# Gate logits of two merges computed between attention items and parked in DRAM; the convolution branch moved up beside merge 2

## The chip, the cores and the metric

One core of a Trainium2 chip runs the whole program. The metric is device time in microseconds from start to end of one execution; the lower, the better. Engines: TensorE (PE, its weight loads PEld), VectorE (DVE), ScalarE (ACT), GpSimd (POOL), SyncE (SP), and 16 DMA engines. Each engine runs its own instructions in order and waits on semaphores.

## The reference

Two layers of a hybrid trunk over 512 latent tokens and 256 context tokens, width 1024, in float32. Each layer normalizes its input to `h`, projects it with `w_in`, and feeds three branches of width 512, whose outputs are merged:

```python
def conv_module(val, glu, z, conv_w, conv_b, ln_g, ln_b):
    a = val * jax.nn.sigmoid(glu)
    a = depthwise_conv(a, conv_w) + conv_b
    return jax.nn.silu(layer_norm(a, ln_g, ln_b)) * jax.nn.silu(z)

def merge_branches(ys, gate_logits, w_branch, w_out):
    y = jnp.stack(ys, axis=2)
    proj = jnp.einsum('btnw,nwd->btnd', y, w_branch)
    gates = jax.nn.sigmoid(gate_logits.reshape(gate_logits.shape[0], gate_logits.shape[1], N_BRANCH, D_MODEL))
    return jnp.sum(gates * proj, axis=2) @ w_out

...
    ys = (y_conv, delta_out(o_dn, dz), diff_out(o_da, az))
    x_new = x + gate[:, None] * merge_branches(ys, mgate, w_branch, w_out)
```

Branch 0 is the convolution (31 taps), branch 1 a chunked gated delta rule in both directions, branch 2 differential attention with four heads. The logits `mgate` are columns of `h @ w_in`: they need nothing of the branches. In the last layer only the latent tokens go on, so most products there have 512 columns and not 768.

## The kernel before

**Items and units.** `schedule()` writes out one list of items, and every engine's program walks this list in order. `units_of(item)` gives the weight units of an item: blocks of 128 x 1024 weights, streamed from DRAM in the order of the list. A dense product is made of three float32r products (high x high, high x low, low x high), so each unit is loaded by SP into `raw`, rounded to `wH` by ScalarE (L754), and its rest `wL` formed by GpSimd (L1684), both in a function `ahead`, which runs up to three units before the unit in use; the ring has four slots, and a slot is reloaded when TensorE is done with the unit before. The products are made in `dense` (L419): a unit has 24 stationary blocks, against 768 columns (two matmuls each) in layer 0 and 512 in most of layer 1.

**Merges.** `merge_steps(l, n)` is four times: gate unit, gate unit, branch unit. A gate's logits stay in a PSUM bank until ScalarE writes their sigmoid to `sg` (L1042). The branch unit gives two products, which VectorE multiplies by `sg` (L1570); for n = 1 into `mT`, otherwise into the single buffer `gm`, which GpSimd adds to `mT` (L1785). The operands of a branch product are `yH` and `yL`, one pair of buffers for all three branches.

**Attention.** The items of head h are `att_steps`: "sc" (scores of a query tile, L466, VectorE's maxima, ScalarE's exponentials L777) and "pv" (transposition L443 of the mixed softmax `Pa`, then the values' product L479 of the tile before). VectorE mixes the softmax of tile i (L1253, L1256) in the "sc" item of tile i+1, the last one in the last "pv". Six query tiles in layer 0, four in layer 1. Between them, `weave` puts a list `side[h]`: the projections of the next head (three units and five short items) and pieces of the merges. Each head ends with "aout": unit az, a sum over the head (L435), ScalarE's reciprocal root and Silu into `vr` (L1157), VectorE's product, `yH` (L1159) and `yL` (L1690).

```python
side = [weave(heads[1], fill[6:]), heads[2], heads[3], merge_steps(l, 2)[:2]]
```

**Tail.** Behind attention stand, one after another: the rest of merge 2 (six gates, four branches) with the layer norm's sum and variance ("lnsum", "lnvar") among it, four z units of the convolution branch, merge 0 (eight gates, four branches), then the output units. In "z" GpSimd scales `acc` by `rsc` (L1794), ScalarE applies Silu (L1068), VectorE multiplies (L1607), ScalarE writes `yH` (L1073), GpSimd `yL` (L1690). VectorE makes the convolution (L1279) in small steps, one at each of many items. Twenty modulation units ("ada", L510) are woven over the whole list in layer 0.

## Time and profile before

| | |
|---|---|
| three runs | 2342.32, 2342.53 and 2440.72 us; median 2342.53 |
| profiled execution | 2335.97 us, span of its instructions 2334.2 us, mean granted clock 0.891 |
| PE busy | 1940.2 us (83%) |
| DVE, ACT, POOL busy | 1077.4 (46%), 986.2 (42%), 778.2 (33%) us |
| DMA | 157.95 MB, mean 68 GB/s |
| weight units | 226, 512 KB each |

The stretches of the table of busy time below are cut where TensorE has finished the sum of an "aout" item. In layer 0 head 0 of attention begins at 635.8 us, head 1 at 760.5, head 2 at 854.5, head 3 at 955.3, and attention's last sum ends at 1033.8; in layer 1 these are 1833.0, 1922.5, 1990.0, 2057.7 and 2111.6. The tail of layer 0 ends at 1285.5 and that of layer 1 at 2273.4. In a row of the timeline stand start, duration, engine, line and operation, and in brackets the engine's idle time before it with what ended it.

### The profile page before, as it was taken

The page shows a single profiled execution, that of the slowest core. Times are in us where ns is not written, and L with a number is a line of the kernel's source. Part 1 is how long each engine was busy: PE and PEld are TensorE (multiplying, and loading weights), DVE is VectorE, ACT ScalarE, POOL GpSimd, SP SyncE. Part 2 cuts the span into 40 slices and gives each one's busy share as a digit, 9 for nine tenths or more (in the row PEclk, how much of TensorE's full clock was granted, in tenths as well). Part 3 has the DMA queues.
Part 4 walks back from the last instruction along what each step waited for, and adds up shares of the span by engine and source line. Part 5 has one row for each costly group of instructions (what it writes and reads, how often), then busy time and mean ns, then how long its engine had stood idle before and what let it go on. Part 6 is the DMA issues. An engine that isn't in the chain of part 4 may idle for free. (4 is left out here: it accounts for less than half of the span.)

```text
span 2334.2 us, 28547 instructions
## 1 busy us (share of the span) xinstructions
PE 1940.2 (83%) x11444; PEld 1623.3 (70%) x11444; DVE 1077.4 (46%) x1592; ACT 986.2 (42%) x1320; POOL 778.2 (33%) x428
## 2 busy tenths in 40 slices
PE   7677896999999877769999767778498997768997
PEld 6665785887887656558888646657487775656876
DVE  3444557358666656421100233547758665541002
ACT  4345652335353544433232234565235545544331
POOL 0122233444434222223554311315145431213562
PEclk8588996799999978779999887989699998889998
DMA  4222222321211101011221312212121210101223
GB/s 176 76 70 64 63 82 73 120 71 46 73 64 55 55 28 46 28 37 54 73 71 65 135 64 64 68 59 91 38 64 56 80 55 28 37 19 58 96 97 111
DMA packets 66194, 157.95 MB, mean 68 GB/s; under 512 B 5328, under 2 KB 28176, under 8 KB 65808
## 3 DMA queue, kind: packets, MB, share of 16 engines
q1 hardware_dynamic: 33264, 122.46, 15.8%
q10 hardware_dynamic: 32800, 33.66, 4.4%
q8 instruction: 93, 1.52, 0.3%
q14 instruction: 37, 0.30, 0.0%
HBM read 145.52 MB, written 10.58 MB: 67 GB/s over the span
## 5 line engine op out<-in xcount | busy, mean ns | idle before, releaser
L1684 POOL TENSOR_TENSOR wL<-raw,wH 128x1024 fp32r<-128x1024 f32 x210 | 523.5, 2496 | 1059.7 <-ACT wH L754 1059.5
L419 PE MATMUL banks<-hH,wH 128*128 128x512 f32 x1984 | 598.6, 363 | 70.4 <-issue 32.9
L419 PE MATMUL banks<-hL,wH 128*128 128x512 f32 x1984 | 581.0, 354 | 0.0
L419 PE MATMUL banks<-hH,wL 128*128 128x512 f32 x1984 | 580.0, 354 | 0.0
L419 PEld LDWEIGHTS banks<-hH,wH 128*128 128x128 f32 x1984 | 327.6, 192 | 135.6 <-issue 74.0
L754 ACT ACTIVATE wH<-raw 128x1024 fp32r<-128x1024 f32 x226 | 237.8, 1054 | 399.3 <-DMA raw<-wstream 399.0
L419 PEld LDWEIGHTS banks<-hL,wH 128*128 128x128 f32 x1984 | 326.2, 192 | 57.2 <-issue 3.9
L419 PEld LDWEIGHTS banks<-hH,wL 128*128 128x128 f32 x1984 | 324.4, 191 | 54.6
L1279 DVE SCALAR_TENSOR_TENSOR acc<-padc,vecs,acc 128x783 f32<-128x783 f32 (+1 forms) x240 | 292.6, 1274 | 0.0
L1570 DVE TENSOR_TENSOR gm<-banks,sg 128x768 f32<-128x768 f32 (+1 forms) x32 | 26.4, 824 | 279.3 <-PE banks L419 218.6
L510 PE MATMUL banks<-wH,csx 128*128 128x128 f32 x384 | 125.7, 350 | 17.4 <-DVE wL L1214 12.1
L777 ACT ACTIVATE Pa<-banks,stat 128x768 f32<-128x768 f32 (+1 forms) x80 | 64.5, 812 | 155.7 <-DVE stat L1240 155.4
L510 PE MATMUL banks<-wL,csx 128*128 128x128 f32 x384 | 123.1, 344 | 0.0
L510 PEld LDWEIGHTS banks<-wH,csx 128*128 128x128 f32 x384 | 99.4, 259 | 20.3 <-issue 13.5
L419 PE MATMUL banks<-yH,wH 128*128 128x512 f32 (+1 forms) x288 | 90.3, 368 | 21.0 <-issue 21.0
L510 PEld LDWEIGHTS banks<-wL,csx 128*128 128x128 f32 x384 | 100.3, 261 | 0.8 <-issue 0.8
L443 PE MATMUL banks<-cons,Pa 128*128 128x128 f32 x208 | 37.5, 323 | 71.5 <-DVE Pa L1256 71.5
L760 ACT ACT_TABLE_LOAD x52 | 66.7, 1283 | 58.3 <-PE banks L435 57.3
L419 PE MATMUL banks<-yL,wH 128*128 128x512 f32 (+1 forms) x288 | 88.5, 362 | 0.0
L419 PE MATMUL banks<-yH,wL 128*128 128x512 f32 (+1 forms) x288 | 88.4, 361 | 0.0
L466 PE MATMUL banks<-kh,qh 64*128 64x256 f32 (+1 forms) x288 | 64.5, 566 | 26.6 <-ACT vr L1157 14.8
L443 PEld LDWEIGHTS banks<-cons,Pa 128*128 128x128 f32 x208 | 28.0, 164 | 82.1 <-issue 81.0
(249 smaller groups left out, 2621.8 us busy)
## 6 DMA issues: line engine op xcount, KB each, us to landing
raw<-wstream SPq DMA_DIRECT2D x226, 512.0 KB, 3.4
E<-g_rows ACTq DMA_DIRECT2D x16, 384.0 KB, 6.9
egb<-eg_rows ACTq DMA_DIRECT2D x20, 256.0 KB, 4.0
inb<-intra_rows ACTq DMA_DIRECT2D x20, 256.0 KB, 4.6
xs<-xT SPq DMA_DIRECT2D x1, 3072.0 KB, 15.4
intra_rows<-E ACTq DMA_DIRECT2D x8, 384.0 KB, 3.3
xs<-xT ACTq DMA_DIRECT2D x1, 3072.0 KB, 13.4
x_between<-xs ACTq DMA_DIRECT2D x8, 384.0 KB, 3.3
```

Source lines behind the costliest of these rows:

```text
L419: last = pe.matmul(out[:, a:b], w, m[:, kt, a:b], start=(kt == 0 and j == 0), stop=(kt == kts - 1 and j == 2))
L443: last = pe.transpose(out[:, c * P:(c + 1) * P], src[:, c * P:(c + 1) * P], ident)
L466: last = pe.matmul(outs[m][:, o:o + b - a], q_[r, qt * P:(qt + 1) * P], k_[r, a:b], start=True, stop=True)
L510: last = pe.matmul(out[:, 0:P], csx[:, 4 * kt:4 * kt + P], w[i][:, kt * P:(kt + 1) * P], start=(kt == 0 and j == 0), stop=(kt == KT - 1 an ...
L754: act.activation(wH[w % RING][:, :], raw[w % RING][:, :], ACT.Copy).then_inc(*tick("act", "hi", v))
L760: ins = act.activation(dst[:, 0:n], place[readkey][:, 0:n], ACT.Ln, bias=e, scale=scale)
L777: act.activation(Pa[i][m][:, 0:w], place[key][:, 0:w], ACT.Exp, bias=stat[:, i, 2 + m:3 + m], accum_out=stat[:, i, 4 + m:5 + m]).then_inc( ...
L1279: ins = dve.scalar_tensor_tensor(acc[:, t, 0:W], padc[:, t, k:k + W], w, acc[:, t, 0:W], ALU.mult, ALU.add)
L1570: dve.tensor_tensor(dst, place[(u, j)][:, 0:n], sg[j][:, 0:n], ALU.mult).then_inc(*tick_read("dve", (u, j)))
L1684: pool.tensor_tensor(wL[w % RING][:, :], raw[w % RING][:, :], wH[w % RING][:, :].bitcast(F32), ALU.subtract).then_inc(*tick("pool", "lo", v))
```

## The change

The sixteen gate units of merges 2 and 0 become items "park", and are woven into heads 1, 2 and 3: four, five and seven. ScalarE copies the logits to `sg` and sends them to DRAM; two parks share the two buffers. Behind attention `park_in` brings two tiles of logits back at a time into four buffers `sgin`, and `sigmoids` is applied in place. The order behind attention is now: "lnsum", z unit 0, "lnvar", z unit 1, the first "ynorm" (the second half of what was "z"), then four branches of merge 2 with the other z units and "ynorm" items between them, then four branches of merge 0. The convolution branch has operand buffers of its own, `yH0` and `yL0`, and merges 2 and 0 have two product buffers `gms`. VectorE makes a convolution step at every gate or park item.

```diff
@@ -118,13 +118,15 @@
                  for h in range(NT)]
         att = [att_steps(l, h) for h in range(NT)]
         fill = merge_steps(l, 1)
-        side = [weave(heads[1], fill[6:]), heads[2], heads[3], merge_steps(l, 2)[:2]]
+        park = [("park", l, n, d) for n in (2, 0) for d in range(KT)]
+        side = [weave(heads[1], fill[6:]), weave(heads[2], park[:4]), weave(heads[3], park[4:9]), park[9:]]
         mid = weave(heads[0], fill[:6])
         for h in range(NT):
             mid += weave(att[h], side[h]) + [("aout", l, h)]
-        rest = merge_steps(l, 2)[2:]
-        mid += rest[:1] + [("lnsum", l)] + rest[1:4] + [("lnvar", l)] + rest[4:]
-        mid += [("z", l, t) for t in range(NT)] + merge_steps(l, 0)
+        mid += [("lnsum", l), ("z", l, 0), ("lnvar", l), ("z", l, 1), ("ynorm", l, 0)]
+        for p in range(4):
+            mid += [("branch", l, 2, p)] + [("z", l, p + 2)] * (p < 2) + [("ynorm", l, p + 1)] * (p < 3)
+        mid += [("branch", l, 0, p) for p in range(4)]
         out += weave(mid, late)
         out += [("out", l)]
     return out
...
...
@@ -320,8 +325,12 @@
 
         padc = arena("padc", [P, NT, PADW], PADC)
         acc = arena("acc", [P, NT, ACCW], ACC0)
-        sqc = [arena("sqc_%d" % i, [P, ACCW], 16 * T3 + i * 3264) for i in range(2)]
+        sqc = [arena("sqc_%d" % i, [P, ACCW], 26 * T3 + i * 3264) for i in range(2)]
         rsc = arena("rsc", [P, TOK], 20 * T3)
+        yH0 = arena("yH0", [P, NT, TOK], 22 * T3, F32R)
+        yL0 = arena("yL0", [P, NT, TOK], 26 * T3, F32R)
+        sgin = [sg[0], sg[1]] + [arena("sgin%d" % i, [P, TOK], (30 + i) * T3) for i in range(2)]
+        gms = [gm, arena("gm1", [P, TOK], 21 * T3)]
         zt = [arena("zt_%d" % i, [P, TOK], 16 * T3 + i * T3) for i in range(4)]
 
         qh = [arena("qh_%d" % i, [P, TOK], (16 + i) * T3) for i in range(2)]
@@ -337,6 +346,7 @@
         csb = arena("csb", [P, KT, 2], 31 * T3 + 1024)
         cs32 = arena("cs32", [P, KT, 2], 31 * T3 + 1088)
 
+        pscr = nc.dram_tensor("parked_logits", (DEPTH, 2, KT, P, TOK), F32, kind="Internal").ap()
         xscr = nc.dram_tensor("x_between", (P, KT, TOK), F32, kind="Internal").ap()
         gscr = nc.dram_tensor("g_rows", (2, NC, NT, P), F32, kind="Internal").ap()
         egscr = nc.dram_tensor("eg_rows", (2, NC, NT, P), F32, kind="Internal").ap()
@@ -655,7 +665,7 @@
                 elif k == "glu":
                     unit(("val", l, it[2]), "val")
                     unit(("glu", l, it[2]), "glu")
-                elif k == "gate":
+                elif k in ("gate", "park"):
                     unit(units_of(it)[0], "gate")
                 elif k == "branch":
                     n, p = it[2], it[3]
@@ -664,7 +674,7 @@
                     for j in range(2):
                         out = product(pe, (u, j), w)
                         pe.wait_ge(*done("y", n, l, NT - 1))
-                        last = dense(u, out, yH, yL, segs(w), NT, j * P, 2 * P)
+                        last = dense(u, out, yH if n else yH0, yL if n else yL0, segs(w), NT, j * P, 2 * P)
                         last.then_inc(*tick("pe", "pe", (u, j)))
                     got[("pe", u)] = got[("pe", (u, 1))]
                 elif k == "lnsum":
@@ -782,6 +792,22 @@
                 for d in range(2):
                     act.dma_start(E[h % 2][:, d, :, :], gscr[d, :, h, :].unsqueeze(0).to_broadcast([P, NC, P])).then_inc(
                         *tick("e_in%d" % (h % 2), "Ein", l, h, d, by=16))
+
+            def park_in(l, n_, p):
+
+                n = ntok(l, "gate")
+                for d in (2 * p, 2 * p + 1):
+                    act.wait_ge(*done("park", l, n_, d))
+                    act.wait_ge(*done("park", l, 0, KT - 2 + d % 2))
+                    act.dma_start(sgin[d % 4][:, 0:n], pscr[l, n_ // 2, d, :, 0:n]).then_inc(
+                        *tick("park_in%d" % (d % 4), "gin", l, n_, d, by=16))
+
+            def sigmoids(l, n_, p):
+
+                n = ntok(l, "gate")
+                for d in (2 * p, 2 * p + 1):
+                    act.wait_ge(*done("gin", l, n_, d))
+                    act.activation(sgin[d % 4][:, 0:n], sgin[d % 4][:, 0:n], ACT.Sigmoid).then_inc(*tick("act", "gsig", l, n_, d))
 
             def scan_in(l, s):
 
@@ -1040,11 +1066,36 @@
                         act.wait_ge(*done(*last_sg[d % 2]))
                     last_sg[d % 2] = ("gm", l, n_, d)
                     act.activation(sg[d % 2][:, 0:n], place[u][:, 0:n], ACT.Sigmoid).then_inc(*tick_read("act", u))
+                elif k == "park":
+                    n_, d = it[2], it[3]
+                    n = ntok(l, "gate")
+                    u = units_of(it)[0]
+                    ahead(u)
+                    act.wait_ge(*done("pe", u))
+                    act.wait_ge(*done(*last_sg[d % 2]))
+                    last_sg[d % 2] = ("park", l, n_, d)
+                    act.activation(sg[d % 2][:, 0:n], place[u][:, 0:n], ACT.Copy).then_inc(*tick_read("act", u))
+                    act.wait_ge(*done("read", u, 0))
+                    act.dma_start(pscr[l, n_ // 2, d, :, 0:n], sg[d % 2][:, 0:n]).then_inc(
+                        *tick("park_out%d" % (d % 2), "park", l, n_, d, by=16))
                 elif k == "branch":
+                    n_, p = it[2], it[3]
                     ahead(units_of(it)[0])
+                    if n_ == 2 and p == 0:
+                        sigmoids(l, 2, 0)
+                    if n_ == 2 or n_ == 0 and p < 3:
+                        sigmoids(l, n_ if p < 3 else 0, (p + 1) % 4)
+                    if n_ == 2 or n_ == 0 and p < 2:
+                        for d in (2 * p, 2 * p + 1):
+                            act.wait_ge(*done("gm", l, n_, d))
+                        park_in(l, n_ if n_ == 2 and p < 2 else 0, (p + 2) % 4)
                 elif k in ("lnsum", "lnvar"):
                     n = ntok(l, "cz")
                     W = ACCW if n == TOK else SEQ
+                    if k == "lnsum":
+                        act.wait_ge(*done("pe", ("o", l, 3, ntok(l, "aq") // P - 1)))
+                        park_in(l, 2, 0)
+                        park_in(l, 2, 1)
                     for t in ((0, 1) if k == "lnsum" else (2, 3)):
                         act.wait_ge(*done("xc", l, t))
                         if t >= 2:
@@ -1058,10 +1109,12 @@
                     u = ("cz", l, t)
                     ahead(u)
                     act.wait_ge(*done("pe", u))
-                    act.wait_ge(*done("rsc", l))
                     if t >= 2:
                         act.wait_ge(*done("y32", 0, l, t - 2))
                     act.activation(zt[t % 2][:, 0:n], place[u][:, 0:n], ACT.Silu).then_inc(*tick_read("act", u))
+                elif k == "ynorm":
+                    t = it[2]
+                    n = ntok(l, "cz")
                     act.wait_ge(*done("xn", l, t))
                     for a, b in segs(n):
                         o = HALO if a else 0
@@ -1069,8 +1122,8 @@
                                          scale=vecs[:, l, V_LG + t:V_LG + t + 1],
                                          bias=vecs[:, l, V_LB + t:V_LB + t + 1]).then_inc(*tick("act", "lns", l, t, a))
                     act.wait_ge(*done("y32", 0, l, t))
-                    act.wait_ge(*done("pe", ("branch2", l, 3)))
-                    act.activation(yH[:, t, 0:n], zt[2 + t % 2][:, 0:n], ACT.Copy).then_inc(*tick("act", "yh", 0, l, t))
+                    act.wait_ge(*done("yl", 2, l, NT - 1))
+                    act.activation(yH0[:, t, 0:n], zt[2 + t % 2][:, 0:n], ACT.Copy).then_inc(*tick("act", "yh", 0, l, t))
                 elif k == "qunit":
                     h, kind = it[2], it[3]
                     u = (kind, l, h)
@@ -1257,7 +1310,7 @@
                                          ALU.mult, ALU.add).then_inc(*tick("dve", "mixp", l, h, qt))
 
             added = set()
-            last_gm = [None]
+            last_gm = [None, None]
             conv_done = [0]
 
             def conv(l, n):
@@ -1559,22 +1612,21 @@
                         u = ("branch%d" % n_, l, p)
                         gu = ("gate%d" % n_, l, d)
                         dve.wait_ge(*done("pe", (u, j)))
-                        dve.wait_ge(*done("read", gu, 0))
+                        dve.wait_ge(*(done("read", gu, 0) if n_ == 1 else done("gsig", l, n_, d)))
                         if n_ == 1:
                             dst = mT[:, d, 0:n]
                         else:
-                            dst = gm[:, 0:n]
-                            if last_gm[0]:
-                                dve.wait_ge(*done(*last_gm[0]))
-                            last_gm[0] = ("gadd", l, n_, d)
-                        dve.tensor_tensor(dst, place[(u, j)][:, 0:n], sg[j][:, 0:n],
+                            dst = gms[j][:, 0:n]
+                            if last_gm[j]:
+                                dve.wait_ge(*done(*last_gm[j]))
+                            last_gm[j] = ("gadd", l, n_, d)
+                        dve.tensor_tensor(dst, place[(u, j)][:, 0:n], (sg[j] if n_ == 1 else sgin[d % 4])[:, 0:n],
                                           ALU.mult).then_inc(*tick_read("dve", (u, j)))
                         got[("gm", l, n_, d)] = got[("read", (u, j), 0)]
                         if n_ == 1:
                             got[("gadd", l, 1, d)] = got[("gm", l, n_, d)]
                 elif k in ("gate", "qunit", "vunit"):
-                    if k != "gate" or it[2] == 1:
-                        conv(l, 1)
+                    conv(l, 1)
                 elif k == "lnsum":
                     conv(l, 2 * CK)
                     n = ntok(l, "cz")
@@ -1592,7 +1644,7 @@
                             got[("xc", l, t)] = got[("read", key, 0)]
                         else:
                             ins.then_inc(*tick("dve", "xc", l, t))
-                elif k == "z":
+                elif k == "ynorm":
                     t = it[2]
                     n = ntok(l, "cz")
                     dve.wait_ge(*done("read", ("cz", l, t), 0))
@@ -1687,7 +1739,8 @@
             def lowy(n_, l, h, n, y32):
 
                 pool.wait_ge(*done("yh", n_, l, h))
-                pool.tensor_tensor(yL[:, h, 0:n], y32[:, 0:n], yH[:, h, 0:n].bitcast(F32), ALU.subtract).then_inc(*tick("pool", "yl", n_, l, h))
+                hi, lo = (yH, yL) if n_ else (yH0, yL0)
+                pool.tensor_tensor(lo[:, h, 0:n], y32[:, 0:n], hi[:, h, 0:n].bitcast(F32), ALU.subtract).then_inc(*tick("pool", "yl", n_, l, h))
                 got[("y", n_, l, h)] = got[("yl", n_, l, h)]
 
             pool.memset(csx[:, KT * 4:].bitcast(F32), 0.0).then_inc(*tick("pool", "csx0"))
@@ -1773,7 +1826,7 @@
                         pool.memset(padc[:, :, :], 0.0).then_inc(*tick("pool", "padz", l))
                     for u in units_of(it):
                         ahead(u)
-                elif k == "gate":
+                elif k in ("gate", "park", "z"):
                     ahead(units_of(it)[0])
                 elif k == "branch":
                     n_, p = it[2], it[3]
@@ -1782,12 +1835,11 @@
                     if n_ != 1:
                         for d in (2 * p, 2 * p + 1):
                             pool.wait_ge(*done("gm", l, n_, d))
-                            pool.tensor_tensor(mT[:, d, 0:n], mT[:, d, 0:n], gm[:, 0:n],
+                            pool.tensor_tensor(mT[:, d, 0:n], mT[:, d, 0:n], gms[d % 2][:, 0:n],
                                                ALU.add).then_inc(*tick("pool", "gadd", l, n_, d))
-                elif k == "z":
+                elif k == "ynorm":
                     t = it[2]
                     n = ntok(l, "cz")
-                    ahead(units_of(it)[0])
                     pool.wait_ge(*done("rsc", l))
                     for a, b in segs(n)[::-1]:
                         o = HALO if a else 0
```

## Rows read from the trace of the kernel before

**Rows 1.** Busy time by stretch, layer 0: length, busy and count, clock, DMA share

```profile
635.80:760.50 124.70, 118.72 (x695) 98.79 (x694) 83.00 (x100) 54.08 (x74) 43.78 (x18) 0.99 0.19 60
760.50:854.50 94.00, 72.51 (x391) 57.17 (x390) 52.61 (x78) 43.09 (x63) 25.26 (x12) 0.89 0.13 40
854.50:955.30 100.80, 80.47 (x409) 64.15 (x408) 55.72 (x80) 44.22 (x65) 26.77 (x13) 0.80 0.13 42
955.30:1033.80 78.50, 57.83 (x307) 46.76 (x306) 32.26 (x62) 33.09 (x51) 13.69 (x6) 0.83 0.10 34
1033.80:1055.50 21.70, 11.12 (x48) 9.59 (x49) 2.93 (x3) 8.19 (x8) 5.97 (x3) 0.69 0.06 22
1055.50:1285.50 230.00, 230.00 (x1319) 198.63 (x1317) 23.68 (x39) 66.60 (x75) 109.52 (x56) 1.00 0.21 68
```

**Rows 2.** Busy time by stretch, layer 1, the same columns

```profile
1833.00:1922.50 89.50, 84.44 (x413) 65.93 (x412) 59.70 (x72) 40.86 (x53) 32.29 (x15) 0.96 0.18 59
1922.50:1990.00 67.50, 53.20 (x269) 41.29 (x268) 35.44 (x52) 34.76 (x47) 16.51 (x10) 0.90 0.10 32
1990.00:2057.70 67.70, 53.91 (x267) 42.02 (x266) 35.57 (x52) 34.77 (x47) 15.84 (x10) 0.85 0.10 31
2057.70:2111.60 53.90, 37.78 (x179) 28.14 (x178) 21.01 (x38) 26.70 (x37) 7.96 (x5) 0.87 0.09 30
2111.60:2128.40 16.80, 7.99 (x25) 6.43 (x26) 2.13 (x3) 7.34 (x8) 5.52 (x4) 0.70 0.10 32
2128.40:2273.40 145.00, 143.40 (x617) 115.07 (x615) 14.93 (x22) 53.24 (x63) 83.98 (x46) 1.00 0.28 91
```

**Rows 3.** Waits of PE, layer 0, 760.5 to 1033.8 (total us, times, longest)

```profile
PE banks L443 <- DVE Pa L1256: 38.0, 11, 5.7
PE banks L466 <- ACT vr L1157: 10.3, 2, 5.1
PE banks L510 <- ACT vr L1157: 5.1, 1, 5.1
```

**Rows 4.** Waits of PE, layer 1, 1922.5 to 2111.6

```profile
PE banks L443 <- DVE Pa L1256: 29.2, 7, 5.7
PE banks L466 <- issue: 5.7, 2, 2.8
PE banks L466 <- ACT vr L1157: 4.5, 1, 4.5
```

**Rows 5.** Busy time by stretch: one gate unit of layer 0, two of layer 1

```profile
983.41:991.84 8.43, 8.43 (x49) 7.44 (x49) 2.34 (x6) 5.20 (x8) 3.40 (x2) 1.00 0.19 62
2224.29:2235.17 10.88, 10.88 (x50) 9.01 (x48) 0.69 (x1) 2.72 (x3) 7.12 (x5) 1.00 0.31 96
```

**Rows 6.** Timeline of PE, layer 0: the first matmul of merge 2's first branch

```profile
1044.38 0.77 PE L419 MATMUL banks<-yH,wH 128*128 128x512 f32 x1 [10.60 <-issue]
```

**Rows 7.** Timeline of PE: the layer norm's sum, layer 0 and layer 1

```profile
1055.51 5.12 PE L435 MATMUL banks<-acc,ones 128*128 128x512 f32 x15
...
2128.26 3.59 PE L435 MATMUL banks<-acc,ones 128*128 128x512 f32 x8
```

**Rows 8.** Timeline of ACT, layer 1: the convolution branch's last heads, then a gate

```profile
2209.41 0.63 ACT L1073 ACTIVATE yH<-zt 128x512 fp32r<-128x512 f32 x1 [0.81 <-DVE zt L1607]
2209.94 1.04 ACT L754 ACTIVATE wH<-raw 128x1024 fp32r<-128x1024 f32 x1
...
2216.67 0.63 ACT L1073 ACTIVATE yH<-zt 128x512 fp32r<-128x512 f32 x1 [0.81 <-DVE zt L1607]
...
2218.27 1.28 ACT L1042 ACT_TABLE_LOAD   x1
2219.56 0.60 ACT L1042 ACTIVATE sg<-banks 128x512 f32<-128x512 f32 x1
```

**Rows 9.** Timeline of ACT, layer 0: one issue of a DMA

```profile
1309.82 0.33 ACTq L1172 DMA_DIRECT2D x_between<-xs  x1
```

**Rows 10.** DMA issues: KB each, median us to landing

```profile
intra_rows<-E ACTq DMA_DIRECT2D x8, 384.0 KB, 3.3
```

3 lines of the change are left out of this document (added).

## Prediction

> **What bounds the kernel now.** I read the table of busy time by stretch first, cut at the output item of each attention head [rows 1, 2]. It shows where TensorE isn't full. Layer 0's tail, from "lnsum" to the end of merge 0, has 230.0 us with PE busy for 230.0, clock 1.00. Layer 1's tail lacks 1.6 us in 145.0. Head 0 of attention, with ten weight units among its items, is nearly full as well: 6.0 us idle in 124.7. Heads 1, 2 and 3 have four, four and three units, and leave 21.5, 20.3 and 20.7 us idle, at clocks of 0.89, 0.80 and 0.83; the 21.7 us between attention and the tail leave 10.6. Layer 1 looks the same: 14.3, 13.8, 16.1 and 8.8 us. So the kernel is bound by TensorE, except where the softmax chain runs with too little beside it.
>
> What a stretch loses I call its excess: length less PE busy, plus busy time by (1 - granted clock), an estimate of what the lower of the two levels (1.2 for 2.4 GHz) costs. Layer 0: heads 21.5+8.0, 20.3+16.1, 20.7+9.8, together 96.4 us, and 10.6+3.4 = 14.0 after them. Layer 1: 14.3+5.3, 13.8+8.1, 16.1+4.9, together 62.5, and 8.8+2.4 = 11.2 [rows 1, 2]. The table of waits says what ends the idle time [rows 3, 4]: the transposition in a "pv" item waits for VectorE's mixed softmax (38.0 us in 11 waits, 3.5 each; layer 1 29.2 in 7, 4.2 each), and the second product behind an "aout" item waits until ScalarE has read that item's banks (15.4 us in three; layer 1 10.2 in three, with those put down to issue).
>
> **The change part by part.** TensorE's work stays the same: every unit, product and column. The sum is made of idle time and clock.
>
> (1) *Gates moved.* Sixteen gate units a layer lie between attention items, where two did; 14 leave a tail that was full, at 8.43 us each in layer 0 and 10.88/2 = 5.44 in layer 1 [rows 5]. Heads 1, 2 and 3 get 4, 5 and 7 of them, in place of 0, 0 and 2. Written out item by item, a "pv" waits only if no unit stands between it and the "sc" item in which VectorE mixes its softmax, or if VectorE has a head sum's result to wait for first. In layer 0 those are three in head 1 (the fourth to sixth query tile), one in head 2 (the fifth), none in head 3; in layer 1 one, one and none. At today's means [rows 3, 4] that is 4 x 3.5 = 13.8 us and 2 x 4.2 = 8.3. The bank wait stays whole (15.4 and 10.2), since the same products stand behind "aout". Of the other small waits (62.5-38.0-15.4 = 9.1 us; layer 1 4.8) I keep 3 and 2, head 0's level. Idle after: 32.2 and 20.5. The clock falls behind idle time: today 33.9 us of clock loss on 62.5 idle (0.54), in layer 1 18.3 on 44.2 (0.41) [rows 1, 2]; by the same ratios 17.4 and 8.4. Excess after: 49.6 and 28.9. **Gain 46.8 + 33.6 = 80.4 us.** A second way, from head 0: three heads like it (7.2 us of excess each, 8.5 in layer 1) and the bank waits with their clock share (23.7, 14.4) give 45.3 and 39.9, a gain of 74.
>
> (2) *What a park adds.* On ScalarE a Copy in place of a Sigmoid of the same size and a DMA issue of 0.33 us [rows 9]. The wait for that write's landing stands two parks later, at least two units (16.9 or 10.9 us) away, against 3.3 us for 384 KB to DRAM on this queue [rows 10]. Behind ScalarE's wait for the unit stand only exponentials that TensorE hasn't prepared either. Cost 0; with the cover gone, 3.3 us a time. On VectorE convolution steps move up with the parks and end in head 2, so head 3's softmax meets none. On GpSimd and SP the weights pass in the new order; ScalarE and GpSimd are at most 46% and 27% busy in these heads [rows 1]. The reads are issued from "lnsum" on, about two branches ahead of use.
>
> (3) *Handover.* The first branch of merge 2 waits 10.6 us for its operand [rows 6]. After the change "lnsum" (5.1 us; 3.6 in layer 1 [rows 7]) and z unit 0 stand before it, and z unit 1 too: this stall and its 3.4 us of clock go. Next late is the variance sum, which waits for squares: in layer 0 it starts 13.5 us behind attention's last sum, and has them; in layer 1 after 9.0 us, where I count 2.3 us of wait (bounds 0 and today's 8.8 [rows 2]).
>
> (4) *The shorter tail.* Merge 0 needs the convolution branch, whose heads go one by one through ScalarE, GpSimd and VectorE. Today this cycle is 7.26 us in layer 1 (2209.41 to 2216.67 [rows 8]). Woven between the branches of merge 2 it takes on two table loads (2 x 1.28), another wH (1.04), two sigmoids (1.2) and two DMA issues (0.7): 12.7 us, while TensorE's work per cycle, a branch and a z unit, is 10.9. TensorE has done "lnsum", two z units and "lnvar" 20 us behind attention's end; the first y comes some 6 us later (end of wH 2210.98 to end of yH 2217.30 [rows 8]), the last one three cycles on, at 64. TensorE has six more units (32.6 us) and asks for it at 53. The last cycle has no z unit in it, so I take 10 us of wait and not 11. With the 2.3 and 0.3 of clock loss per us of idle, as at the handover today (2.4 on 8.8): 16.0 us of excess, against 11.2+1.6 today. In layer 0 the steps that grow with the columns (12.7 less loads, wH, its wL and the issues: at most 6 us, by at most 768/512) add under 3 us: 15.7, under TensorE's 16.9. Only the last y is late there, about 2.7 us, with the clock 4.0. What the second product buffer of merges 2 and 0 gives before the output units I take at 0. **Layer 0: 14.0 - 4.0 = 10; layer 1: 12.8 - 16.0 = -3.**
>
> In this chain the change adds switches of ScalarE's table. The rows show a load of 1.28 us whose sigmoid starts 0.01 us behind it: a switch costs 1.28 here [rows 8].
> The Trainium skill (ScalarE: Activation LUTs, "What ACT_TABLE_LOAD costs") puts a drain of about 1.38 us on each switch; by that rule the cycle of layer 1 would be 15.5 us and that of layer 0 18.5, and the sum some 13 us worse. The trace doesn't agree.
>
> **Sum.** 80.4 + 10 - 3 = 87 us. The profiled execution took 2335.97 us (span 2334.2), which gives 2249; the runs' median is 2342.53, 6.6 more, so I forecast 2255, 3.7% down.
>
> **The rivals.**
> *Full cover* (0.10): no "pv" waits, and layer 1's chain keeps up. That is 22 us of waits, 11 of clock and 16 of the tail more: 2206. For it: head 0's clock of 0.99. Against: head 0 still idles 6 us, with ten units.
> *Only head 3 gains* (0.15): in heads 1 and 2 the head sums and rotations keep the waits where they are. Layer 0 gains 30.5-9.4 = 21, layer 1 21.0-7.3 = 14, the rest 7: 42 us, 2300. Against it: head 0, with the same small items.
> *Costly switches* (0.05): each table load drains ScalarE before the next step. At one more load's length per switch (1.28 [rows 8]), eight in layer 1's chain and the last cycle of layer 0: 13 us, 2268.
> *Slower: the trip to DRAM* (0.04): ScalarE, in order, stands in a DMA wait with the softmax behind it. All 64 transfers at 3.3 us would be 211 us: 2466. It decides from 1.4 us per transfer on the path (87/64). That needs landings several times longer than today's [rows 10], as two units lie between a write and the wait for it.
> *No effect* (0.02): the stretches keep their idle time although units lie in them: 2342.
> The forecast keeps 0.64.
>
> **Range and chances.** The forecast's own spread is the number of "pv" waits (2 to 8 a layer, 5 us each with clock) and layer 1's tail (0 to 20 us): 2225 to 2285. The range 2222 to 2300 takes in costly switches and nearly all of "only head 3"; full cover's end and the slower case stay out. 2% (47 us) is about what a measurement of this kernel can tell from no change; that line is at 2296. Faster 0.80 (forecast, full cover, switches, a little of the third), within 0.16, slower 0.04.
>
> **What would show it.** Heads 1 to 3 longer by their gates, with PE idle 10 to 14, 8 to 11 and 5 to 7 us and a clock of 0.92 or more; the bank wait unchanged in each; no wait behind the last head's sum; one wait of some 10 us at the first branch of merge 0 in layer 1, ended by GpSimd's yL, and 3 us in layer 0. I am wrong if merge 2's branches wait for sigmoids, if weights come late behind the new traffic, or if heads 1 and 2 still idle 20 us.

## The result, and the profile after

The changed kernel takes **2265.92 us** (median of four runs, 2263.15 to 2271.35) beside 2343.4 for the kernel before on the same chip: ratio 0.9681, 95% interval 0.9658 to 0.9704. The ratio is of runs in the fast state alone; one of the four of the kernel before (2440.72 us) was slower and isn't in it. The forecast was 2255, in a range of 2222 to 2300. The two profiled executions have spans of 2269.6 and 2334.2 us, 64.6 apart; the account below is made on them. The medians lie about 77 us apart, since the profiled execution of the kernel before was 7 us faster than its median and that of the changed kernel 5 us slower; the gains by spans below come out smaller by that much.

Busy time by stretch of the changed kernel, layer 0: head 0, heads 1 to 3, the tail from "lnsum" to the end of merge 0, and the time up to the output units. Columns as in [rows 1].

```profile
635.56:765.09 129.53, 120.86 (x695) 100.28 (x694) 82.96 (x101) 54.21 (x74) 42.94 (x18) 0.97 0.19 58
765.09:890.66 125.57, 109.53 (x600) 90.16 (x599) 56.97 (x80) 51.34 (x73) 37.52 (x17) 0.90 0.20 64
890.66:1019.66 129.00, 114.90 (x647) 95.50 (x646) 58.01 (x80) 53.20 (x75) 40.22 (x18) 0.93 0.21 69
1019.66:1123.30 103.64, 94.22 (x565) 78.89 (x565) 43.35 (x64) 39.91 (x60) 28.35 (x12) 0.98 0.25 83
1123.30:1246.50 123.20, 119.01 (x660) 101.57 (x658) 25.52 (x38) 63.67 (x71) 77.63 (x43) 0.97 0.34 112
1246.50:1260.85 14.35, 0.35 (x3) 0.24 (x3) 11.32 (x13) 8.03 (x11) 6.28 (x3) 0.55 0.75 282
```

Layer 1: heads 1 to 3 and the tail. Compare [rows 2].

```profile
1886.54:1972.47 85.93, 73.98 (x363) 57.34 (x363) 35.98 (x52) 41.38 (x55) 25.56 (x14) 0.92 0.20 62
1972.47:2060.99 88.52, 80.68 (x387) 62.67 (x386) 35.76 (x52) 43.05 (x57) 28.63 (x15) 0.94 0.22 69
2060.99:2127.75 66.76, 61.05 (x299) 47.51 (x299) 23.11 (x38) 31.04 (x44) 20.52 (x10) 0.97 0.30 91
2127.75:2210.30 82.55, 74.64 (x305) 57.76 (x303) 16.43 (x25) 51.98 (x63) 56.16 (x36) 0.96 0.39 127
```

Length less the first busy column is the idle time: 16.0, 14.1 and 9.4 us in the heads of layer 0 (before 21.5, 20.3 and 20.7), 12.0, 7.8 and 5.7 in layer 1 (14.3, 13.8 and 16.1). The units are where they should be: PE's matmuls in the three heads of layer 0 went from 391, 409 and 307 to 600, 647 and 565. The excess, worked out as in the prediction (in the column "after", idle time and clock loss):

| stretch | before | predicted | after | gain predicted | gain measured |
|---|---|---|---|---|---|
| heads 1 to 3, layer 0 | 96.4 | 49.6 | 39.5 + 20.9 = 60.4 | 46.8 | 36.0 |
| heads 1 to 3, layer 1 | 62.5 | 28.9 | 25.5 + 12.6 = 38.1 | 33.6 | 24.4 |
| handover and tail, layer 0 | 14.0 | 4.0 | 4.2 + 3.6 = 7.8 | 10 | 6.2 |
| handover and tail, layer 1 | 12.8 | 16.0 | 7.9 + 3.0 = 10.9 | -3 | 1.9 |
| head 0, layer 0 | 7.2 | 7.2 | 8.7 + 3.6 = 12.3 | 0 | -5.1 |
| before the output units, layer 0 | 11.9 | 11.9 | 14.0 | 0 | -2.1 |

Together 61 of the 64.6 us; the stretches outside the table give 1 us, and the rest is within the rounding of the clock column. What PE waited for in heads 1 to 3, layer 0:

```profile
PE banks L429 <- ACT vr L1210: 10.3, 2, 5.1
PE banks L453 <- DVE Pa L1309: 7.9, 2, 4.2
PE banks L476 <- ACT vr L1210: 5.1, 1, 5.1
PE banks L453 <- ACT Pa L787: 4.7, 1, 4.7
PE banks L489 <- ACT Pa L787: 3.4, 2, 2.4
PE banks L453 <- ACT adar L844: 2.4, 2, 2.0
```

and in layer 1:

```profile
PE banks L453 <- DVE Pa L1309: 10.8, 2, 8.0
PE banks L476 <- issue: 5.9, 2, 3.1
PE banks L476 <- ACT vr L1210: 4.6, 1, 4.6
```

The first line of the first list says: products of L429 (a weight unit) waited twice for banks that ScalarE's `vr` step of L1210 had to read, 10.3 us in all, 5.1 at most. The wait for VectorE's softmax fell from 38.0 us in 11 to 7.9 in 2 [rows 3], and in layer 1 from 29.2 in 7 to 10.8 in 2 [rows 4]. The wait for az's banks (ACT vr) stands as it was, 5.1 us each time in layer 0. The wait of 10.6 us at merge 2 [rows 6] is gone. New in the list is a wait for "adar", ScalarE's copy of an ada unit's result.

### The profile page after: what moved, and what is told of

The parts are those of the page before. It is cut to its first block and busy times, and to the rows that moved or that the text cites. A ratio compares the mean times of both kernels' runs of the same rounds, so it can differ in the third digit from the quotient of the medians.

```text
span 2269.6 us, 28683 instructions
## 1 busy us (share of the span) xinstructions
PE 1919.4 (85%) x11444; PEld 1605.1 (71%) x11444; DVE 1103.4 (49%) x1592; ACT 1009.9 (44%) x1354; POOL 778.2 (34%) x428
## 5 line engine op out<-in xcount | busy, mean ns | idle before, releaser
L429 PE MATMUL banks<-hH,wH 128*128 128x512 f32 x1984 | 604.2, 366 | 83.5 <-issue 31.8
L429 PE MATMUL banks<-hL,wH 128*128 128x512 f32 x1984 | 584.6, 356 | 0.0
L429 PE MATMUL banks<-hH,wL 128*128 128x512 f32 x1984 | 584.1, 356 | 0.0
L429 PEld LDWEIGHTS banks<-hH,wH 128*128 128x128 f32 x1984 | 331.1, 194 | 151.6 <-issue 75.5
L429 PEld LDWEIGHTS banks<-hL,wH 128*128 128x128 f32 x1984 | 329.2, 193 | 57.5 <-issue 4.1
L429 PEld LDWEIGHTS banks<-hH,wL 128*128 128x128 f32 x1984 | 327.3, 192 | 54.7
L1332 DVE SCALAR_TENSOR_TENSOR acc<-padc,vecs,acc 128x783 f32<-128x783 f32 (+1 forms) x240 | 304.3, 1325 | 0.0
L520 PE MATMUL banks<-wH,csx 128*128 128x128 f32 x384 | 118.7, 336 | 11.1 <-DVE wL L1267 11.0
L520 PE MATMUL banks<-wL,csx 128*128 128x128 f32 x384 | 117.4, 333 | 0.0
L520 PEld LDWEIGHTS banks<-wH,csx 128*128 128x128 f32 x384 | 94.8, 247 | 14.0 <-issue 12.5
L429 PE MATMUL banks<-yH,wH 128*128 128x512 f32 (+1 forms) x288 | 89.8, 366 | 11.0 <-issue 11.0
L429 PE MATMUL banks<-yL,wH 128*128 128x512 f32 (+1 forms) x288 | 87.7, 358 | 0.0
L429 PE MATMUL banks<-yH,wL 128*128 128x512 f32 (+1 forms) x288 | 87.6, 358 | 0.0
L453 PE MATMUL banks<-cons,vb 128*128 128x128 f32 x48 | 12.1, 425 | 81.7 <-ACT vb L926 81.7
L770 ACT ACT_TABLE_LOAD x52 | 66.7, 1283 | 32.2 <-PE banks L445 31.5
L1409 DVE TENSOR_SCALAR c<-pad,vecs 128x769 f32<-128x769 f32 (+1 forms) x24 | 46.1, 1922 | 65.3 <-ACT pad L913 65.3
L1290 DVE TENSOR_REDUCE stat<-banks 128x1 f32<-128x768 f32 (+1 forms) x80 | 64.1, 842 | 26.2 <-PE banks L476 26.2
```

The lines of the kernel that those rows point to most:

```text
L429: last = pe.matmul(out[:, a:b], w, m[:, kt, a:b], start=(kt == 0 and j == 0), stop=(kt == kts - 1 and j == 2))
L453: last = pe.transpose(out[:, c * P:(c + 1) * P], src[:, c * P:(c + 1) * P], ident)
L520: last = pe.matmul(out[:, 0:P], csx[:, 4 * kt:4 * kt + P], w[i][:, kt * P:(kt + 1) * P], start=(kt == 0 and j == 0), stop=(kt == KT - 1 an ...
L770: ins = act.activation(dst[:, 0:n], place[readkey][:, 0:n], ACT.Ln, bias=e, scale=scale)
L1290: dve.tensor_reduce(stat[:, i, m:m + 1], place[key][:, 0:w], AX_X, ALU.max).then_inc(*tick("dve", "mx", l, h, qt, m))
L1332: ins = dve.scalar_tensor_tensor(acc[:, t, 0:W], padc[:, t, k:k + W], w, acc[:, t, 0:W], ALU.mult, ALU.add)
```

## The experiments

Twelve kernels ran, each in three rounds beside the kernel before, in groups of four that shared a chip (its median 2338.5, 2338.99 and 2338.71 us there). Ratios are to the kernel before; the changed kernel has 0.9681 (0.9658 to 0.9704). Lines of code are cut where "..." stands.

### Gates and tail, each alone

First the tail in its new order with the gates still in it:

```diff
-        side = [weave(heads[1], fill[6:]), weave(heads[2], park[:4]), weave(heads[3], park[4:9]), park[9:]]
+        side = [weave(heads[1], fill[6:]), heads[2], heads[3], merge_steps(l, 2)[:2]]
...
+            mid += g2[2 * p:2 * p + 2] * (p > 0) + [("branch", l, 2, p)]
```

> The new tail alone: the convolution branch has its own operand buffers and its items stand beside merge 2, but no gate is parked; the gate units stay before their branches as in the kernel before. My theory (most of the gain is made by units that fill idle time between attention items, the rest at the handover): the heads stay as they were, the wait of 10.6 us behind the last head's sum and its clock loss go in layer 0, most of 11 us in layer 1, and the convolution chain is hidden by the gates beside it: about 2318 us, 25 less than before. Rival: the gain came from the tail's order and buffers, the parked gates only moved work from one full place to another: 2266 to 2285. Second rival: the tail gives nothing alone: 2343.

Measured: 2307.79 us, 0.9871 (0.9853 to 0.9888), 10 us under the expectation. The heads didn't stay as they were, though no gate moved: in layer 0 heads 0 and 1 are 4.2 and 3.1 us longer than before, head 2 is 8.7 shorter (92.1 for 100.8) and head 3 3.7. The ada units had moved here too, see below, and one of them (some 2 us) out of head 2; that this is the cause was not run by itself. Its tail in layer 0 has no idle time:

```profile
1029.00:1260.00 231.00, 231.00 (x1325) 200.19 (x1324) 25.81 (x43) 74.03 (x84) 113.95 (x58) 1.00 0.21 67
```

Then the gates parked, with the tail in its old order:

```diff
...
+        mid += [("lnsum", l), ("branch", l, 2, 0), ("branch", l, 2, 1), ("lnvar", l), ("branch", l, 2, 2), ("branch", l, 2, 3)]
+        for t in range(NT):
+            mid += [("z", l, t), ("ynorm", l, t)]
...
```

> The parked gates with the tail in the old order: sum, two branches, variance, two branches, then the four heads of the convolution branch in a row, then merge 0. My theory: PE idle in the heads as in the changed kernel; behind attention a wait of 5 us comes back (the sum covers half of 10.6), and in layer 1 the four z units (5.4 us each) are shorter than the chain's cycle (7.3 us), so merge 0 waits some 8 to 10 us instead of 6.8; in layer 0 hardly anything else: 2275 to 2285 us. Rival (the order of the tail carries the gain): above 2310. Rival (the order is worth nothing): 2266.

Measured: 2297.97 us, 0.9818 (0.9799 to 0.9836), 13 us above the expectation's upper end. Its heads are those of the changed kernel; its tails, layer 0 and 1:

```profile
1120.90:1254.80 133.90, 118.89 (x645) 100.11 (x644) 24.83 (x37) 58.76 (x67) 76.26 (x42) 0.95 0.31 102
2140.90:2236.30 95.40, 77.68 (x305) 59.95 (x303) 16.98 (x25) 47.03 (x59) 55.89 (x36) 0.89 0.33 110
```

15.0 and 17.7 us idle, where the changed kernel has 4.2 and 7.9. The wait of some 5 us for merge 2's operand came back, as expected (5.5 and 5.4); what was missed is the wait at merge 0, 9.2 us in layer 0, where next to none was expected, and 11.6 in layer 1. The two parts add up: 1.29% and 1.82% make 3.11, beside 3.19 for both. A tail without its gates no longer covers the convolution branch's chain, so the new order is worth some 30 us there.

### Which pv items wait

Units put directly before the pv items of heads 1 and 2 (the same units in all):

```diff
...
+            gap = {6: [[q], [k, qs], [v], [qr, units[0]], [ks, units[1]], [vt, units[2]]],
+                   4: [[q, k], [qs, v], [qr, ks, units[0]], [vt, units[1]]]}[n]
+            for qt in range(n):
+                out += [("sc", l, h, qt + 1)] * (qt + 1 < n) + gap[qt] + [("pv", l, h, qt)]
...
```

> The changed kernel with the side items of heads 1 and 2 placed by hand, in both layers: the same items, but a weight unit stands directly before each pv item where the order allows it, the small items (head sums, rotations, turn) ahead of it. My theory (what is left idle in these heads is pv items without a unit before them): the 7.9 us of layer 0 and the 10.8 us of layer 1 that TensorE waits for the mixed softmax go, with their clock loss: 25 to 30 us less than the changed kernel, about 2240. Rival (the rest is due to banks not yet read by ScalarE, whose place in the order I don't change): 2266 within 5 us.

Measured: 2260.67 us, 0.9668 (0.9645 to 0.969), not to be told from the changed kernel, and near the rival's value, not my 2240. Waits of PE in its heads 1 to 3, layer 0:

```profile
PE banks L489 <- ACT vr L1223: 15.4, 3, 5.1
PE banks L442 <- ACT Pa L800: 7.8, 4, 2.0
```

Head 1 has 10.6 us idle for 16.0, head 2 13.9 for 14.1. No pv waits for VectorE any more, as expected, but now the units (L442) wait for banks that ScalarE hasn't read. Here the place of the units decided which item waits, and most of the idle time stayed.

### Where the ada units stand

The late ada units of layer 0 are woven over a list that the four new "ynorm" items make longer (130 places for 126), so that they stand up to one item later than before in head 0, one or two in head 1 and two or three in heads 2 and 3. Spread as in the kernel before:

```diff
-        out += weave(mid, late)
+        groups = []
+        for it in mid:
+            if it[0] == "ynorm":
+                groups[-1].append(it)
+            else:
+                groups.append([it])
+        out += [it for g in weave(groups, [[it] for it in late]) for it in g]
```

> The changed kernel, with its late ada units spread as in the kernel before: the four new ynorm items don't count as places in the list over which they are woven. My theory of head 0 in layer 0, which got 4.8 us longer (129.5 for 124.7): the new items shift the ada units among the attention items, and two of them now stand before pv items of head 0. Then head 0 takes 125 us again, the wait for ScalarE's adar (1.4 us) goes, and the time is some 5 us down, 2261. Rival: the parked traffic or the Copy instead of Sigmoid disturbs head 0 (it can't from a later place in ScalarE's order, but weights come earlier), then it stays at 129.5.

Measured: **2251.96 us**, 0.9616 (0.9592 to 0.964), better than the changed kernel beyond both intervals, and 14 us where 5 were expected. Heads 0 to 3 of layer 0:

```profile
635.80:760.50 124.70, 119.48 (x695) 99.61 (x694) 85.37 (x101) 54.08 (x74) 42.54 (x18) 0.97 0.19 60
760.50:877.20 116.70, 104.22 (x601) 86.86 (x600) 60.70 (x80) 51.48 (x73) 38.23 (x17) 0.96 0.21 68
877.20:1002.60 125.40, 112.37 (x649) 93.58 (x648) 58.38 (x80) 53.46 (x75) 40.55 (x18) 0.96 0.21 71
1002.60:1108.60 106.00, 96.78 (x565) 80.95 (x565) 42.98 (x64) 39.82 (x60) 28.23 (x12) 0.94 0.24 81
```

Head 0 takes 124.7 us again. That isn't chance: in seven other kernels here with the changed kernel's spacing it takes 128.0 to 130.4 us, and in the two at the end that have the old one 124.6 and 124.9 (in the kernel before with Silu first, old spacing too, 127.3 with no more idle time, at a clock of 0.96 for 0.99). The excess of heads 1 to 3 is 16.6 + 17.5 + 15.0 = 49.2 us, where the changed kernel has 60.4: 34.7 us idle for 39.5, and 14.5 of clock loss for 20.9. The other way round, with these units taken out of heads 1 to 3 and put behind "lnsum" (one is left, at the start of head 1):

```diff
...
+            out += weave(mid[:cut], late[:6]) + mid[cut:end] + weave(mid[end:], late[6:])
...
```

> The changed kernel, with the ada units that lay in heads 1 to 3 of layer 0 moved behind lnsum, into the tail. My theory: where ada units stand decides how much idle time the heads have; the earlier spacing gained 14 us, as its units stood before pv items. With none of them in heads 1 to 3 the pv waits that they covered come back, some 2 us of unit and its switch each, 11 units: heads 1 to 3 shorter by the units' own 24 us but with 10 or more us more idle time and clock loss, the tail 24 us longer with no wait at merge 0; 2270 to 2285 in all. Rival: ada units among attention items cost more than they cover (each makes a head's items wait for ScalarE's adar); then the heads' idle time stays or falls and the time is under 2262.

Measured: 2257.28 us, 0.9646 (0.9612 to 0.9679): what the rival expected, and not the 2270 of my theory. Heads 1 to 3 of layer 0:

```profile
759.20:874.50 115.30, 100.78 (x551) 82.14 (x549) 57.99 (x74) 47.88 (x67) 30.07 (x14) 0.91 0.18 56
874.50:991.30 116.80, 104.12 (x579) 85.71 (x578) 53.99 (x72) 48.76 (x67) 30.45 (x14) 0.96 0.18 58
991.30:1089.20 97.90, 89.70 (x513) 74.53 (x513) 37.89 (x58) 36.43 (x54) 20.99 (x9) 0.95 0.22 72
```

The heads' excess is 23.6 + 16.8 + 12.7 = 53.1: less than the changed kernel's 60.4, more than the 49.2 with the units in the old places. The idle time alone is 35.4 us here, 39.5 in the changed kernel and 34.7 in the old places: ada units in the old places covered next to nothing, and in the new places they cost some 4 us. I had held that any ada unit covers some idle time; that fell. That a unit at the wrong item delays it by its own work and its copy on ScalarE is my reading of the waits for "adar" (2.4 us), not shown by a run.

### The wait for az's banks

Silu of az ahead of the reciprocal root in "aout", in the changed kernel and in the one before:

```diff
-                    rsqrt(None, at1[1], 1.0 / P, eps, ("aors", l, h), ("oss", l, h), n)
                     act.wait_ge(*done("pe", u))
                     act.activation(vr[:, 0:n], place[u][:, 0:n], ACT.Silu).then_inc(*tick_read("act", u))
+                    rsqrt(None, at1[1], 1.0 / P, eps, ("aors", l, h), ("oss", l, h), n)
```

> The changed kernel, with the Silu of az moved ahead of the reciprocal root in each aout item, so that the product behind it gets its banks earlier. My theory: the wait for ScalarE's reading of these banks (5.1 us three times in layer 0, some 3.4 three times in layer 1) is a loss of its own, beside the pv waits, and carries its share of the clock: idle time of heads 1 to 3 falls by 15 and 10 us, excess by some 23 and 14, and the time from 2266 to about 2232. Rival: ScalarE is the chain behind aout anyway, and the time reappears as a wait of the next pv for VectorE's softmax or ScalarE's exponentials; then less than 12 us are gained and the pv waits grow by what the bank wait loses.

Measured: 2260.2 us, 0.9645 (0.9624 to 0.9665), 6 us less than the changed kernel by the medians, the intervals just touching; the rival expected that, and my theory 34 us.

> The kernel before, with the same edit (Silu of az ahead of the reciprocal root in aout). If the bank wait is independent of how many gate units lie in the heads, as the prediction had it, this gains the same 25 us of idle time and a share of the clock, some 35 us: 2305 beside 2338. If the chain of the softmax takes it up, which is more likely here as nothing else stands behind aout, under 15 us: above 2324.

Measured: 2339.81 us, 0.9993 (0.9974 to 1.0013): no change. PE behind the "aout" of head 2 in layer 0, first in the kernel before, then with the edit:

```profile
961.96 2.93 PE L466 MATMUL banks<-kh,qh 64*128 64x512 f32 x8 [5.14 <-ACT vr L1157]
969.96 1.30 PE L443 MATMUL banks<-cons,Pa 128*128 128x128 f32 x5 [5.07 <-DVE Pa L1256]
```

```profile
959.17 1.56 PE L466 MATMUL banks<-kh,qh 64*128 64x512 f32 x8 [1.74 <-ACT at L760]
970.26 1.09 PE L443 MATMUL banks<-cons,Pa 128*128 128x128 f32 x4 [9.52 <-DVE Pa L1256]
```

The bank wait falls by 3.4 us and the next pv's grows by 4.5: the transposition starts at the same time (14.6 and 14.3 us behind the head's sum). It was slack in front of the softmax. With units between, a part of it is real: heads 1 and 2 of layer 0 became 6.6 and 6.8 us shorter in the changed kernel, while a unit's wait of 6.4 us for ScalarE's exponentials took the place of one of the three.

### What sets the tail's chain

First the table switches: Sigmoid in place of both Silu of the z and ynorm steps, so that ScalarE switches no table between them and the gates' sigmoids (the convolution branch's activation is then another).

```diff
-                    act.activation(zt[t % 2][:, 0:n], place[u][:, 0:n], ACT.Silu)...
+                    act.activation(zt[t % 2][:, 0:n], place[u][:, 0:n], ACT.Sigmoid)...
...
```

> The changed kernel with Sigmoid in place of both Silu functions of the convolution branch, so that ScalarE needs no table switch between its steps and the gates' sigmoids in the tail (this changes what is computed, and nothing else of the order). My theory (the last cycles of the convolution chain are what merge 0 waits for, with two loads of 1.28 us in each): layer 1's cycle falls from 12 to about 9.5 us, under TensorE's 10.9, and the wait of 6.8 us at merge 0 goes to 2 or less, layer 0's 4.2 to 3: 8 to 10 us less than the changed kernel. If a switch cost a drain too, twice that. Rival (the wait is GpSimd's, its wL and sums in order): no change within 3 us.

Measured: 2270.19 us, 0.9705 (0.969 to 0.9721): nothing gained. ScalarE's loads between these steps are gone, and `yH` still comes every 11.9 us (2147.63, 2159.58 and 2171.51 us). The wait at merge 0, layer 1, in the changed kernel and in this one:

```profile
2186.77 0.77 PE L429 MATMUL banks<-yH,wH 128*128 128x512 f32 x1 [6.77 <-issue]
```

```profile
2183.30 0.77 PE L429 MATMUL banks<-yH,wH 128*128 128x512 f32 x1 [6.58 <-issue]
```

GpSimd in the changed kernel, one cycle of the chain:

```profile
2165.04 2.40 POOL L1736 TENSOR_TENSOR wL<-raw,wH 128x1024 fp32r<-128x1024 f32 x1
2167.39 2.55 POOL L1838 TENSOR_TENSOR mT<-mT,gm 128x512 f32<-128x512 f32 x2
2169.90 2.39 POOL L1736 TENSOR_TENSOR wL<-raw,wH 128x1024 fp32r<-128x1024 f32 x1
2172.24 1.09 POOL L1846 TENSOR_TENSOR acc<-acc,rsc 128x512 f32<-128x512 f32 x1
2175.71 1.30 POOL L1743 TENSOR_TENSOR yL<-zt,yH 128x512 fp32r<-128x512 f32 x1 [2.38 <-ACT yH L1126]
```

It is busy for 9.7 us and waits 2.4 for one round through ScalarE and VectorE: 11.9 us from one yL (2163.79) to the next, with small overlaps. So I took the two additions (L1838) from it and gave them to VectorE:

```diff
...
-                            pool.tensor_tensor(mT[:, d, 0:n], mT[:, d, 0:n], gms[d % 2][:, 0:n], ...
+                            dve.tensor_tensor(mT[:, d, 0:n], mT[:, d, 0:n], gms[d % 2][:, 0:n], ...
```

> The changed kernel, with the additions of merges 2 and 0 to mT on VectorE in place of GpSimd. My theory now: in layer 1's tail GpSimd's order of work (a wL of 2.4, two additions of 1.27, a wL of 2.4, xn 1.1, yL 1.3) sets the cycle of the convolution branch, not ScalarE. Without the additions it falls by some 2.5 us per head: the wait of 6.8 us at merge 0 in layer 1 shrinks to under 1.5, layer 0's 4.2 to about 3 (it is put down to adar), and the time falls by some 7 to 10 us, 2257. Rival: ScalarE's order (sigmoids, wH, norm steps, yH) sets it, and the wait stays within 1.5 us of 6.8.

Measured: 2264.69 us, 0.9669 (0.9639 to 0.9698), not to be told from the changed kernel by its time. In the trace the wait is nearly halved, the cycles are 12.2, 10.4 and 8.2 us, and the tail of layer 1 is 3.5 us shorter:

```profile
2179.48 0.76 PE L429 MATMUL banks<-yH,wH 128*128 128x512 f32 x1 [3.69 <-issue]
```

GpSimd's order does bind, but the wait was expected under 1.5 us and is 3.7: both engines' operations got longer where they met. Two such additions took VectorE 2.06 us at 2203.49, and 4.13 us here:

```profile
2160.84 2.87 POOL L1741 TENSOR_TENSOR wL<-raw,wH 128x1024 fp32r<-128x1024 f32 x1
```

```profile
2160.12 4.13 DVE L1631 TENSOR_TENSOR mT<-mT,gm 128x512 f32<-128x512 f32 x2
```

The same trace has a second gain that I hadn't expected: PE's wait before the output units fell from 11.1 to 9.0 us in layer 0 and from 10.7 to 7.6 in layer 1. With 3.1 us at merge 0 that is 8 of the 9 us by which the profiled span is shorter; the medians, 1 us apart with intervals of some 14 us, can't confirm it.

### The trip to DRAM

Each parked gate written twice, both writes awaited:

```diff
...
+                    act.dma_start(pscr2[l, n_ // 2, d, :, 0:n], sg[d % 2][:, 0:n]).then_inc(
+                        *tick("park_twice%d" % (d % 2), "park2", l, n_, d, by=16))
...
```

> The changed kernel, with every parked gate written to DRAM a second time (to another tensor, on the same queue); the buffer is reused, and the reads begin, only when both writes have landed. The output is the same. The prediction had the price of a park at 0, since two units lie between a write and the wait for it: then the time stays within 4 us of 2266, as 32 more DMA issues on ScalarE and 11 MB are beside TensorE's work. Rival, the trip to DRAM: the landings take up what is gained; 32 more transfers at 3 to 4 us would add tens of us, 2290 or more, and weights would come late.

Measured: 2274.17 us, 0.9716 (0.9684 to 0.9748), 8 us more than the changed kernel by the medians, where at most 4 were expected, with overlapping intervals, and a profiled span of 2270.3 beside 2269.6. By the medians that is a quarter of a microsecond for each of 32 writes; no stretch of the trace shows it, so whether it is there stays open. The second writes of layer 0 (384 KB each) land 4.8 us behind their issue in the median.

### Together

The ada units' old spacing, Silu first and the additions on VectorE, with the units before the pv items too, and without them:

> What gained by itself, together: ada units spread as before, units placed directly before the pv items of heads 1 and 2, Silu of az ahead of the reciprocal root, additions of merges 2 and 0 on VectorE. If the gains add up (14 + 5 + 6 + 6 us by their medians) it gives 2266 - 31 = 2235. If they are the same idle time counted twice (a wait removed by one returns as the next one in the chain of the softmax), about the best of them, 2250.

Measured: 2244.39 us, 0.9591 (0.9556 to 0.9625), between the 2235 of a plain sum and the 2250 of the best edit alone.

> As the run before, without the placing of units before the pv items. 2266 - 26 = 2240 if the gains add up; beside the run before it shows what the placing is worth once no product behind aout waits for az's banks: 5 us, or less if the ada units have already given head 1 its cover.

Measured: **2232.93 us**, 0.9534 (0.9498 to 0.9569), the fastest, 7 us under the plain sum's 2240, 33 us below the changed kernel and 106 below the one before. The three edits together give more than what they gave alone by their medians (14 + 6 + 1), which with intervals of some 10 us each is no contradiction to a plain sum. The placing of units, 5 us by itself and inside the intervals, costs 11 on top of them (the intervals of the two ratios overlap by a hair, but the slowest of the four runs without it, 2234.44, lies below the fastest with it, 2239.82). Heads 1 and 2, layer 0, of the fastest:

```profile
761.40:873.20 111.80, 103.33 (x599) 86.50 (x598) 60.93 (x80) 50.23 (x73) 38.12 (x17) 0.95 0.22 71
873.20:992.70 119.50, 110.46 (x647) 92.26 (x646) 60.46 (x80) 52.07 (x75) 39.52 (x18) 0.97 0.23 74
```

8.5 and 9.0 us idle in heads 1 and 2. With the units placed they are 13.1 each, and what PE waits for there is a unit's banks behind ScalarE's exponentials, 20.7 us in five waits over heads 1 to 3:

```profile
PE banks L448 <- ACT Pa L806: 20.7, 5, 6.4
```

## Why the prediction was right, and where it was off

The forecast's case held, and its time lies 11 us above. By the spans the sum of 87 us became 64.6, by the medians about 77.

(1) *Gates moved.* Right in kind: heads 1, 2 and 3 gain, most where most gates went. The idle time was mis-sized, 39.5 us for 32.2 in layer 0 and 25.5 for 20.5 in layer 1, and the signs that the prediction named for it were missed in layer 0: 16.0, 14.1 and 9.4 us for 10 to 14, 8 to 11 and 5 to 7, and a clock of 0.90 in head 1 for 0.92 or more. In layer 1 (12.0, 7.8 and 5.7 us) they came about. Term by term:

| idle time | predicted, layer 0 | measured | predicted, layer 1 | measured |
|---|---|---|---|---|
| pv items behind the softmax | 13.8 (4 waits) | 12.6 (3) | 8.3 (2) | 10.8 (2) |
| az's banks | 15.4 | 15.4 | 10.2 | 10.5 |
| all other waits | 3 | 11.5 | 2 | 4.2 |

So in layer 0 the step that failed in size is the term of the other small waits, which I had put at head 0's level: they didn't shrink as more units came. Of the 11.5 us, 2.4 are the new waits for "adar", at two pv items. The prediction left the ada units where they were, and the diff moves them, by lengthening the list they are woven over. Put back, heads 1 to 3 have 49.2 us of excess, and head 0 its 124.7. That this meets the predicted 49.6 is in part luck: it is 34.7 of idle time and 14.5 of clock loss, where 32.2 and 17.4 were predicted.

In layer 1, which has no ada units, 5.0 us of idle time and 4.2 of clock loss are missing; one pv waits 8.0 us there. The trace shows what was late. VectorE first waits for ScalarE's root of a head sum, as in the kernel before, and then makes two convolution steps ahead of the last mixture. Beside them GpSimd now forms the weight difference of a parked gate:

```profile
1948.33 2.35 POOL L1736 TENSOR_TENSOR wL<-raw,wH 128x1024 fp32r<-128x1024 f32 x1 [10.05 <-ACT wH L764]
1948.47 3.41 DVE L1332 SCALAR_TENSOR_TENSOR acc<-padc,vecs,acc 128x512 f32<-128x512 f32 x2
```

The same two steps in the kernel before, with GpSimd idle, and a pv wait of 5.7 us behind them:

```profile
1973.23 1.41 DVE L1279 SCALAR_TENSOR_TENSOR acc<-padc,vecs,acc 128x512 f32<-128x512 f32 x2
```

These 2.0 us are nearly all by which that wait grew. The prediction moved GpSimd's weight differences beside the softmax at no price. In heads 1 to 3 of layer 0 VectorE's busy time rose from 140.6 to 158.3 us with four more operations; how much of PE's idle time comes of that, no run separates.

What the prediction said of the bank wait was right in number and wrong in weight: it counted 25.6 us of it (38 with clock) as a loss that remains. The runs show that in the kernel before nothing was to be had by taking it away (0.9993), since the next pv waited instead, and after the change about 6 us.

(2) *What a park adds.* On the DMA's side cost 0 held as far as the trace shows. The waits of ScalarE for the parked reads, heads and tail of layer 0:

```profile
ACT sgin L810 <- DMA sgin<-parked_logits: 1.5, 1, 1.5
ACT sg L810 <- DMA sg<-parked_logits: 0.7, 1, 0.7
```

"The trip to DRAM" is refuted as the case of a slower kernel: ScalarE waits 2.2 us for the reads here and 0.2 in layer 1, and doubling the writes moved the median by 8 us, inside the intervals. A price of some us for all of them stays possible.

(3) *Handover.* The 10.6 us went, and in layer 1 the variance sum waits 1.1 us for 2.3.

(4) *The shorter tail.* The cycle was predicted at 12.7 us and is 12.2 and 11.9 (yH at 2150.91, 2163.08 and 2175.00 us); the wait at merge 0 is 6.8 for 10 in layer 1, 4.2 for 2.7 in layer 0, each ending 0.1 us behind GpSimd's last yL, as forecast. But the prediction made the cycle up of ScalarE's table loads, sigmoids and DMA issues, and that was wrong: without the switches it is the same. GpSimd's order, with the two additions and two weight differences in each cycle, sets it. The right number came from the wrong engine, which was luck. In the kernel before it was GpSimd's cycle already: from yL at 2203.05 to yL at 2210.11 it works 4.8 us and waits 2.4. With one more weight difference and two additions (2.4 and 2.6 us) that gives the 12 us. The last cycle has one weight difference less (9.7 us, yH at 2184.70), hence the shorter wait.

"Costly switches" falls with it. ScalarE in the tail of layer 1:

```profile
2151.45 1.04 ACT L764 ACTIVATE wH<-raw 128x1024 fp32r<-128x1024 f32 x1
2152.51 1.28 ACT L810 ACT_TABLE_LOAD   x1
2153.80 1.16 ACT L810 ACTIVATE sg<-sg 128x512 f32<-128x512 f32 x2
```

The load begins 0.02 us behind the activation's end, and the sigmoid 0.01 us behind the load's. A drain of about 1.38 us for each switch, as the Trainium skill has it (ScalarE: Activation LUTs, "What ACT_TABLE_LOAD costs"), doesn't show.

"Only head 3 gains" was half right for the kernel as it is: head 1 gained 2.5 of its 29.5 us of excess in layer 0 and 1.7 of 19.6 in layer 1. Head 2 did gain, 14.3 and 9.2 us. "Full cover" was far off: the best version still has 8 to 10 us idle in each head. Not in the prediction at all: head 0 of layer 0 (5.1 us, the ada units again) and the 2.1 us before the output units, of which the last section tells.

## What to carry to other kernels

A list over which other work is spread by position is part of a change: whoever adds items to it moves everything woven in, and a unit of 2 us at the wrong item can cost more than it covers. A wait that stands in front of a longer chain may be no loss until that chain has cover; take it away alone in the old kernel and see whether the next wait grows by as much. And a cycle that sums to the right length on one engine is not thereby that engine's: add up the others in the same window first.
